# Expert rows gathered by token number: one layer of a hybrid attention, RG-LRU and MoE encoder

## The reference, cut to what matters

```python
g_sel = argmax(x @ w_router_group + b_router_group)            # 1 of 4 groups
e_logits = (x @ w_router_expert + b_router_expert)[group g_sel]  # 4 experts in it
top_vals, top_idx = top_k(e_logits, 2)
p_exp = softmax(top_vals) * p_group                            # gates of the two experts
for e in range(16):
    g, u = split(x @ w_gate_up[e])                             # 1024 -> 2 * 256
    y = y + gate[:, e] * ((silu(g) * u) @ w_down[e])           # 256 -> 1024
tokens = layer_norm(ALPHA * tokens + y)
```

## Time and profile before

| | |
|---|---|
| time, median of 3 runs | 1664.73 us (1663.65 to 1673.5) |
| the profiled execution's own time | 1661.35 us |
| its span in the trace | 1659.5 us |
| TensorE matrix products busy | 1496.0 us, 90% of the span |
| VectorE, ScalarE, POOL busy | 876.7, 531.9, 434.4 us |
| mean granted clock of TensorE | 0.956 of full speed |
| moved by DMA | 204.08 MB, mean 123 GB/s |

### The profile page before, as it was taken

How to read it: one execution, slowest core, us unless ns; L and a number is a source line. 1 busy time by engine, 2 the same in 40 slices (tenths; PEclk the granted TensorE clock), 3 DMA queues, 4 the chain that set the end, 5 groups by cost and what they waited for, 6 DMA issues and landing times.

```text
span 1659.5 us, 24972 instructions
## 1 busy us (share of the span) xinstructions
PE 1496.0 (90%) x10014; PEld 1344.0 (81%) x10014; DVE 876.7 (53%) x1648; ACT 531.9 (32%) x960; POOL 434.4 (26%) x465
## 2 busy tenths in 40 slices
PE   5989999999999899899999998999994299999990
PEld 5976679899999567789899897999994288888880
DVE  4025827999996577431546465443265034434445
ACT  4224542211111565520465655011011022222225
POOL 0744534813233000013334343231100302111110
PEclk7999999999999899999999999999998599999995
DMA  5111010232232830853111111244015768888946
GB/s 190 37 30 29 26 45 16 66 114 82 81 105 72 247 87 25 314 178 91 35 46 42 45 36 47 88 170 150 30 77 200 277 209 228 247 249 277 265 120 247
DMA packets 138089, 204.08 MB, mean 123 GB/s; under 512 B 14676, under 2 KB 89396, under 8 KB 137984
## 3 DMA queue, kind: packets, MB, share of 16 engines
q1 hardware_dynamic: 131808, 180.53, 33.6%
q0 software_dynamic: 6176, 22.10, 5.6%
HBM read 143.99 MB, written 58.61 MB: 122 GB/s over the span
## 4 chain that ended last, share of the span: by engine, by line
PE 76%; DMA 10%; DVE 5%; POOL 4%; issue 2%; ACT 2%; SPq 1%; POOLq 0%; DVEq 0%; ACTq 0%
PE psum L544 18%; PE psum L546 17%; PE psum L545 17%; DMA w_gate_up<-in_w_gate_up 5%; PE psum L1326 5%; PE psum L1140 3%; DMA x_and_experts_by_token<-expert_out,row_token 2%; PE psum L1130 2%; PE psum L1009 2%; PE psum L1162 2%; PE psum L1111 2%; POOL x_by_expert L935 1%; PE psum L1278 1%; PE psum L1318 1%; POOL roped L899 1%
## 5 line engine op out<-in xcount | busy, mean ns | idle before, releaser
L544 PE MATMUL psum<-x_hi,ring_hi 128*128 128x384 f32 x768 | 259.0, 337 | 0.5 <-ACT v L1518 0.5
L546 PE MATMUL psum<-x_lo,ring_hi 128*128 128x384 f32 x768 | 256.6, 334 | 0.0
L545 PE MATMUL psum<-x_hi,ring_lo 128*128 128x384 f32 x768 | 256.5, 334 | 0.0
L905 POOL CAST ring_hi<-ring_raw 128x512 fp32r<-128x512 f32 x88 | 67.1, 763 | 582.3 <-PE psum L546 415.8
L1326 PE MATMUL psum<-expert_rows_T,w_gate_up 128*128 128x192 f32 x1024 | 176.4, 333 | 13.2 <-DMA w_gate_up<-in_w_gate_up 11.8
L1326 PEld LDWEIGHTS psum<-expert_rows_T,w_gate_up 128*128 128x128 f32 x1024 | 171.9, 195 | 17.5 <-issue 8.4
L544 PE MATMUL psum<-w_hi,x_hi 128*128 128x256 f32 x576 | 174.0, 302 | 6.5 <-DVE channel_vectors L1781 3.7
L545 PE MATMUL psum<-w_hi,x_lo 128*128 128x256 f32 x576 | 165.3, 287 | 0.0
L546 PE MATMUL psum<-w_lo,x_hi 128*128 128x256 f32 x576 | 165.1, 287 | 0.0
L544 PEld LDWEIGHTS psum<-x_hi,ring_hi 128*128 128x128 f32 x768 | 144.2, 188 | 1.7 <-ACT v L1518 0.7
L545 PEld LDWEIGHTS psum<-x_hi,ring_lo 128*128 128x128 f32 x768 | 144.2, 188 | 1.1
(11 more groups left out here) (335 smaller groups left out, 3039.3 us busy)
## 6 DMA issues: line engine op xcount, KB each, us to landing
w_gate_up<-in_w_gate_up SPq DMA_DIRECT2D x16, 2048.0 KB, 14.1
ring_raw<-in_w_in SPq DMA_DIRECT2D x64, 256.0 KB, 3.4
w_down<-in_w_down SPq DMA_DIRECT2D x16, 1024.0 KB, 7.5
expert_rows<-x_by_expert SPq DMA_DIRECT2D x16, 774.0 KB, 5.5
x_by_expert<-zeros SPq DMA_DIRECT2D x7, 1536.0 KB, 16.2
gate_sigmoid<-sigmoid_out SPq DMA_DIRECT2D x15, 576.0 KB, 3.2
w_raw<-in_w_in SPq DMA_DIRECT2D x16, 512.0 KB, 4.4
k_cache<-in_cache_k SPq DMA_DIRECT2D x8, 1024.0 KB, 6.0
```

The costliest lines, as they stand in the source:

```text
L544: nc.tensor.matmul(out, ah, bh, start=first, stop=False)
L545: nc.tensor.matmul(out, al, bh, start=False, stop=False)
L546: return nc.tensor.matmul(out, ah, bl, start=False, stop=last)
L905: link(g.tensor_copy(RHI[:, p_ % 2, :, :], RRAW[:, p_ % 2, :, :]))
```

## The change

- x1 is stored a second time, by token, into a DRAM table X1D, whose row 0 is zero (token numbers begin with 1); the table of sums gets 96 more spare rows. The row buffer XS, its zero fills, the scatter and the eight extra columns are gone.
- `route` gives each (token, choice) its position within its expert (POSF). `mark_slots` compares it with 0 to 191 (AT_SLOT, six instructions of 128 x 576). TensorE multiplies AT_SLOT with the 0/1 rows times token number: 36 products of 128x96 weights and 16 columns (`row_table`), then once more with the gates. The result is the token number and the gate of every slot of all 16 experts (GIDX, ROWT, ROWG).
- The running count over tiles is one scan in place of nine steps; the gates come after the token table.
- POOL gathers the rows of expert e + 2 from X1D with two indirect DMAs, ahead of the adds of expert e. SP loads weights only. `row_columns` is gone from VectorE's loop, which is written out; the wait on landed adds moves to `expert_out`, two experts later.

The diff, cut to its core (the old lines of `route`, tables and the branch for overflow are left out):

```diff
-    XS = nc.dram_tensor("x1_by_expert", (E * TOK, DP), f32, kind="Internal").ap()
-    XS_1 = XS[0:E * MS, :].rearrange("(e h p) d -> e p h d", e=E, h=2)
...
-    YSUM = nc.dram_tensor("x1_and_experts_by_token", (1 + TOK + MR, D), f32, kind="Internal").ap()
-    FILLS = [YSUM[1 + TOK:, :].rearrange("p (a b) -> p a b", b=256)]
...
-    FILLS += [flat[:, n * i // 8:n * (i + 1) // 8, :] for i in range(8)]
+    X1D = nc.dram_tensor("x1_by_token", (1 + TOK, D), f32, kind="Internal").ap()
+    YSUM = nc.dram_tensor("x1_and_experts_by_token", (1 + TOK + 2 * MR, D), f32, kind="Internal").ap()
+    FILLS = [YSUM[1 + TOK:1 + TOK + MR, :].rearrange("p (a b) -> p a b", b=256)]
+    FILLS += [YSUM[1 + TOK + MR:, :].rearrange("p (a b) -> p a b", b=256)]
+    FILLS += [X1D[0:1, :].rearrange("p (a b) -> p a b", b=256)]
...
+        lg, le = LG[:, :, 0:4], LG[:, :, 4:20].rearrange("p t (q i) -> p t q i", q=4)
+        lm, tmp, hot = G16[:, 0, :, :], G16[:, 1, :, :], G16[:, 2:4, :, :]
+        def over_experts(x):
+            return x.unsqueeze(3).broadcast_to([128, 2, TT, E])
         first_max(lg, G1[:, 0, :], G4[:, 3, :, :], G1[:, 1, :], G4[:, 0, :, :], PRIO[:, 16:20], 4)
         v.tensor_tensor(G4[:, 1, :, :], lg, bc(G1[:, 0, :], 4), ALU.subtract).then_inc(s_route_steps, 1)
...
+        link(v.tensor_scalar(G4[:, 3, :, :], G4[:, 0, :, :], 1.0, BIG, ALU.subtract, ALU.mult))
+        link(v.tensor_tensor(lm.rearrange("p t (q i) -> p t q i", q=4), le,
+                             G4[:, 3, :, :].unsqueeze(3).broadcast_to([128, TT, 4, 4]), ALU.add))
+        first_max(lm, G1[:, 6, :], tmp, G1[:, 7, :], hot[:, 0, :, :], PRIO[:, 0:16], 16)
+        link(v.scalar_tensor_tensor(lm, hot[:, 0, :, :], -3.0 * BIG, lm, ALU.mult, ALU.add))
+        first_max(lm, G1[:, 8, :], tmp, G1[:, 7, :], hot[:, 1, :, :], PRIO[:, 0:16], 16)
+        link(v.tensor_tensor(PER_E[:, :, :].rearrange("p e t -> p t e"), hot[:, 0, :, :], hot[:, 1, :, :], ALU.add))
+        v.tensor_tensor_scan(UPTO[:, :, :].rearrange("p e t -> p (e t)"), SMASK, PER_E[:, :, :].rearrange("p e t -> p (e t)"),
+                             0.0, ALU.mult, ALU.add).then_inc(s_route_steps, 1)
+        v.tensor_tensor(G1[:, 4, :], G1[:, 8, :], G1[:, 6, :], ALU.subtract).then_inc(s_route_steps, 1)
+        v.tensor_tensor(HOT_TOKEN[:, :, :, :], hot, over_experts(TOKEN[:, :].unsqueeze(1).broadcast_to([128, 2, TT])), ALU.mult)
+        dve.wait_ge(s_route_products, 1)
+        pos = PS[:, 5, 0:E * TT].rearrange("p (e t) -> p t e", e=E).unsqueeze(1).broadcast_to([128, 2, TT, E])
+        link(v.tensor_tensor(G16[:, 0:2, :, :], hot, pos, ALU.mult))
+        link(v.tensor_reduce(POSF[:, :, :], G16[:, 0:2, :, :], AX.X, ALU.add))
+        mark_slots(v)
+        dve.wait_ge(s_route_products, 2)
+        tokens = PS[0:MR, 2:4, 0:E]
+        v.tensor_copy(GIDX[:, :, :], tokens).then_inc(s_rows_known, 1)
+        link(v.scalar_tensor_tensor(ROWU[:, :, :], tokens, 0.0, SPARE[:, :].unsqueeze(2).broadcast_to([MR, 2, E]),
+                                    ALU.is_equal, ALU.mult))
+        v.tensor_tensor(ROWT[:, :, :], ROWU[:, :, :], tokens, ALU.add).then_inc(s_rows_known, 1)
+        dve.wait_ge(s_route_exp, 1)
         link(v.tensor_reduce(G1[:, 2, :], G4[:, 2, :, :], AX.X, ALU.add))
         link(v.reciprocal(G1[:, 3, :], G1[:, 2, :]))
...
+        dve.wait_ge(s_route_exp, 2)
         link(v.tensor_scalar(G1[:, 9, :], G1[:, 5, :], 1.0, ALPHA, ALU.add, ALU.mult))
         link(v.reciprocal(G1[:, 9, :], G1[:, 9, :]))
...
+        link(v.tensor_tensor(GATES[:, 0, :], G1[:, 9, :], G1[:, 3, :], ALU.mult))
+        link(v.tensor_tensor(GATES[:, 1, :], GATES[:, 0, :], G1[:, 5, :], ALU.mult))
+        link(v.tensor_reduce(NMAXF[:, :], PS[:, 5, TT * E:TT * E + E], AX.X, ALU.max))
+        v.tensor_tensor(HOT_GATE[:, :, :, :], hot, over_experts(GATES[:, :, :]), ALU.mult).then_inc(s_at_slot, 1)
+        v.tensor_copy(NMAX[:, :], NMAXF[:, :]).then_inc(s_rows_known, 1)
+        dve.wait_ge(s_route_products, 3)
+        link(v.tensor_copy(ROWG[:, :, :], PS[0:MR, 6:8, 0:E]))
+    def mark_slots(v):
         for c in range(2):
...
+            for t in range(0, TT, 3):
+                v.tensor_tensor(AT_SLOT[:, c, t:t + 3, :], IOTA.unsqueeze(1).broadcast_to([128, 3, MS]),
+                                POSF[:, c, t:t + 3].unsqueeze(2).broadcast_to([128, 3, MS]), ALU.is_equal).then_inc(s_at_slot, 1)
...
                 sp.wait_ge(s_x1, t + 1)
+                sp.dma_start(X1D[1 + 128 * t:1 + 128 * t + 128, :], YACC[:, t, 0:D]).then_inc(s_x1_kept, 16)
                 sp.dma_start(YSUM[1 + 128 * t:1 + 128 * t + 128, :], YACC[:, t, 0:D]).then_inc(s_sums_begun, 16)
...
-            sp.wait_ge(s_scat, 16 * 2 * TT)
-            for e in range(2):
-                sp.dma_start(XG[:, e, :, :], XS_1[e]).then_inc(s_expert_rows_loaded[e], 16)
...
-                if not isinstance(e, int) or e + 3 < E:
-                    sp.wait_ge(s_expert_rows_turned, 4 * e + 8)
-                    sp.wait_ge(s_row_columns, 2 * e + 4)
-                    sp.dma_start(XG[:, 1 - par, :, :], of(XS_1, e + 3)).then_inc(s_expert_rows_loaded[1 - par], 16)
                 if not isinstance(e, int) or e + 2 < E:
                     sp.wait_ge(s_down_lo, e + 1)
                     sp.dma_start(WD[par][:, :, :], of(WD_D, e + 2)).then_inc(s_down_loaded[par], 16)
                     sp.wait_ge(s_gate_up_products, e + 1)
                     sp.dma_start(WG[par][:, :, :], of(WG_D, e + 2)).then_inc(s_gate_up_loaded[par], 16)
...
-            sp.wait_ge(s_expert_rows_turned, 4)
-            sp.wait_ge(s_row_columns, 2)
-            sp.dma_start(XG[:, 0, :, :], of(XS_1, 2)).then_inc(s_expert_rows_loaded[0], 16)
...
+            def gather_rows(e, par, column, done):
+                for h in range(2):
+                    g.indirect_dma_start(XG[:, par, h, :], None, X1D, bass.IndirectOffsetOnAxis(GIDX[:, h, column:column + 1], 0)
+                                         ).then_inc(done, 16)
+            def add_rows(par, h, column, done):
+                g.indirect_dma_start(YSUM, bass.IndirectOffsetOnAxis(ROWT[:, h, column:column + 1], 0), YE[:, par, h, :], None,
+                                     compute_op=ALU.add).then_inc(done, 16)
             pool.wait_ge(s_fill, 16 * len(FILLS))
-            for t in range(TT):
-                for c in range(2):
-                    g.indirect_dma_start(XS, bass.IndirectOffsetOnAxis(SLOT[:, c, t:t + 1], 0), YACC[:, t, :], None
-                                         ).then_inc(s_scat, 16)
-            def add_rows(par, h, done):
...
+            pool.wait_ge(s_x1_kept, 16 * TT)
+            pool.wait_ge(s_states_stored, 16 * 4)
+            pool.wait_ge(s_rows_known, 1)
+            for e in range(2):
+                gather_rows(e, e, e, s_expert_rows_loaded[e])
+            pool.wait_ge(s_rows_known, 2)
             pool.wait_ge(s_sums_begun, 16 * TT)
             for e in range(E):
+                if e + 2 < E:
+                    pool.wait_ge(s_expert_rows_turned, 4 * e + 4)
+                    gather_rows(e + 2, e % 2, e + 2, s_expert_rows_loaded[e % 2])
                 wait(pool, s_expert_out_kept[1 - e % 2], 32 * ((e + 1) // 2))
                 for h in range(2):
                     pool.wait_ge(s_expert_out, 4 * e + 2 * h + 2)
-                    add_rows(e % 2, h, s_expert_out_kept[e % 2])
+                    add_rows(e % 2, h, e, s_expert_out_kept[e % 2])
...
-            pe.wait_ge(s_route_steps, 3)
-            mm(PS[:, 5, 0:TT * E], BEFORE[:, :], G16[:, 5, :, :].rearrange("p t e -> p (t e)"), start=True, stop=False)
-            mm(PS[:, 5, 0:TT * E], ONES[:, :], G16[:, 6, :, :].rearrange("p t e -> p (t e)"), start=False, stop=True)
-            mm(PS[:, 5, TT * E:TT * E + E], ONES[:, :], G16[:, 7, 0, :], start=True, stop=True).then_inc(s_route_replies, 1)
+            pe.wait_ge(s_route_steps, 2)
+            mm(PS[:, 5, 0:TT * E], BEFORE[:, :], PER_E[:, :, :].rearrange("p e t -> p (e t)"), start=True, stop=False)
+            mm(PS[:, 5, 0:TT * E], ONES[:, :], UPTO[:, :, :].rearrange("p e t -> p (e t)"), start=False, stop=True)
+            mm(PS[:, 5, TT * E:TT * E + E], ONES[:, :], UPTO[:, :, TT - 1:TT].rearrange("p e t -> p (e t)"),
+               start=True, stop=True).then_inc(s_route_products, 1)
+            def row_table(values, bank, c0, marked):
+                for c in range(2):
+                    for t in range(TT):
+                        if t % 3 == 0 and marked is not None:
+                            pe.wait_ge(s_at_slot, marked + 3 * c + t // 3 + 1)
+                        for h in range(2):
+                            last = mm(PS[0:MR, bank + h, c0:c0 + E], AT_SLOT[:, c, t, MR * h:MR * h + MR], values[:, c, t, :],
+                                      start=(c, t) == (0, 0), stop=(c, t) == (1, TT - 1))
+                return last
+            row_table(HOT_TOKEN, 2, 0, 0).then_inc(s_route_products, 1)
+            pe.wait_ge(s_at_slot, 7)
```

(64 more changed lines are left out.)

194 lines of the change are left out of this document (75 added, 119 removed).

## The result

The changed kernel takes 1721.39 us (median of 4 runs, 1714.26 to 1724.57) where the kernel before takes 1664.45 (median of 4): a ratio of 1.033, 95% interval 1.031 to 1.035. It is slower, where 1623 was forecast. Its profiled execution took 1720.58, with a span of 1718.7 against 1659.5: 59.2 more.

A forecast was written before the change was run, and what follows sets the result against it. TensorE, busy 90% of the span, was taken as the bound, losing time before the first turn and to w_gate_up. 24.2 + 1.0 + 16.1 = 41.3 off 1661.35 gave 1620.1, forecast as 1623 from the median; range 1613 to 1642.

The forecast's parts named there:

- C: Expert loop: waits for w_gate_up go, gathers late by 0.1 us for 14 experts; 16.1 us gained, 17.5 at most.
- rival one: Expert loop: gathers share DMA with weight loads, land in 7.6 us, each late by 1.4; 1641.6 us; chance 0.20.
- rival three: Turns of 14 experts: POOL's gather much dearer than a plain load, landing above 9.5 us; at 3.8 late 1719; chance 0.04.
- T: Expert loop: the end of the second half of expert e, from which starts of gathers and needs are counted.
- POOL can't start sooner: Expert loop: the argument given for rival one, whose late gathers had a chance of 0.20.
- A: Path from logits to the first turn of expert rows: 24.2 us gained, bounds 5.6 and 28.1.
- B: Clock of the first half expert: 1.0 us gained, between 0 and 2.1.
- the path to the counts: Routing, in A: VectorE's shorter chain gives TensorE its counts at 1272.6, 4.3 us earlier than before.
- the six marks: Routing, in A: VectorE's marks of 576 elements take 0.76 us each, the first at 1276.0, the sixth at 1279.7.
- the gate table decides: Routing, in A: the gate table ends at 1292.1, later than the gather at 1290.5, and sets the first turn.
- the lower bound of the token table: Routing, in A: TensorE ends the table with the last mark, near 1280.5, where 1282.5 was taken.
- A loss is excluded: First half expert, in B: it can't get slower, since TensorE is at the low clock there already.

The follow-up runs named there:

- e2: Changed kernel, with SP loading an expert's w_down and w_gate_up only after that expert's gathered rows have landed; 1637.11 us.
- e6: Changed kernel, with VectorE's one instruction for the low part of w_down split into four; 1688.03 us.
- e1: Changed kernel, with POOL gathering the rows of expert e + 3 in place of e + 2, a beat earlier; 1634.02 us, 0.980 of the kernel before.
- e5: e1 plus ten idle matrix products of 512 columns keeping TensorE at work ahead of the tables; 1626.71 us, 0.977 of the kernel before.
- e3: Changed kernel, with each add moving 16 rows of 96, the other 80 left out of the sums; 1718.78 us.

## Why the prediction was wrong

**C failed, in the landing of the gather.** Of the 100.5 us between the forecast (41.3 less) and the two profiles (59.2 more), C is 84.1. The step "A plain load takes 5.5, an add on POOL's own queue 6.5. I take 6.5" set a landing of 6.5; it is 9.2. The rows that I took it from were of transfers with little beside them, or with one weight load. Here `w_down` and `w_gate_up` of e + 2 go out within 1 us of the second half, which I named in rival one and priced at 7.6. e2 shows that these loads are the whole difference: 5.1 without them. The clock behind the waits, 1.9 a beat, stood in rival three only and at nothing in the forecast. The Trainium skill ("DMA: Bandwidth & Descriptors", Queues, rings and completion order) lets each DMA engine take turns between queues packet by packet; the trace agrees that the gather has to share (5.1 alone, 9.2 beside them), but it pays 4.1 us for it, where the half rate of rival one gave 2.1. The DMA queues' view says where the rest comes from: POOL's queue has 38.2% of the engines from 1461 to 1464 us and moves 0.35 MB, 51.6% from 1464 to 1467 and moves 0.42 MB, so 0.12 to 0.14 MB in a microsecond; with the loads held, in e2, it has 97.6% from 1461.9 to 1463 and moves 0.34 MB in these 1.1 us. Even alone it is slower than the 384 GB/s that rival one halved.

**C failed, too, in the start of the second half**, T - 1.1 from the scatters' distance of 1.27 us: it is T + 0.26, since VectorE's 2.29 us instruction stands across the first half (e6). The scatters that I took the 1.27 from ran with VectorE idle. The formula was right, two of its terms were not: with e2's terms, 0.27 + 5.08 - 5.3, it gives 0.05, and e2 has no wait there. And "POOL can't start sooner", in rival one, holds for the rows of e + 2 only: e1 asks for each expert's rows a beat sooner.

**Rival three came true, with the cause of rival one.** Its price, 3.8 us of lateness, and its time, 1719, are nearly what was measured (4.65 a wait on average; 1721.39); its extra 3.1 for the clock is 1.9. That its time is so near is luck in part: it has the loop lose 79.1, where 68.0 is measured, and what A, B and the end fall short of the forecast, 14.1 together, happens to make up for it. I gave it 0.04 because I saw no reason for a dear gather; by itself a gather is cheap (5.1), and it is dear beside the loads. (13 gathers are late and not 14: that of the third expert goes out with no add ahead of it.) The landing from which it decides was given as above 9.5 us with the second half at T - 1.1; at the measured start it is 8.1, and 9.2 is above that. A slack of zero (late by 0.1) on 14 repeated steps should have had more weight than 0.04 for the slow side: each microsecond of error was worth 14 us.

**A was mis-sized, by 9.6 of 24.2**, in the pair of weight load and product: 0.09 taken, 0.1625 measured, two tables of 72, 10.4 us. The eight pairs of the earlier trace rows ran at a granted clock of 1.00; the tables run at 1.2 GHz. The price that the Trainium skill ("TensorE: Matmul & The Clock Gate", LDWEIGHTS) gives, by an estimate from it 0.08 for 96 columns, agrees with the 0.09 of e5 at the high clock; at the low one the trace has 0.1625, twice that. Right were the path to the counts (6.56 us behind the logits, 6.5 forecast), the six marks (4.10, forecast 4.6), the gather ahead of the turn, and that the gate table decides.

(In the lower bound of the token table it should say that TensorE is never faster than the marks; its number stands.)

**B**: -0.5, outside 0 to 2.1; the clock is still down when the half expert begins (0.50 from 1307 to 1310 us). "A loss is excluded" was wrong, but where the same tables take 7.0 to 8.1 us from one profile to the next, one pair of profiles can't tell a B of this size.

**Right**: no wait for `w_gate_up`, the beat of 17.3 once the rows are there (e1), the fills, the stores and the tail's work costing nothing that TensorE's waits show. e1 gets the 32.6 us that A, B and C give with the rows in time (14.6 + 0.5, with its first half expert of 7.00, + 17.5) and keeps 30.4 of it, since the end takes 2.2 longer.

**Open**: the end behind the last add is 43.5 us here and 40.5 before. ScalarE waits 3.39 us for the second sums in place of the 1.50 before. With the same tail e5 takes 40.8 and e6 44.7, so the change need not be the reason. No run was made for it, nor for the moving start of the routing, nor for the lower clock of e3.

## What to carry to other kernels

A step with no slack that is repeated for each expert puts the whole loop at stake: work out what each microsecond of error costs before choosing between two rows, and read the price of a DMA from a row with the same loads beside it. When a load moves to another queue, list everything that goes out within its landing time, on all queues. Before paying for a faster transfer, issue it one beat earlier: that cost a few lines here and was worth 87 us (e1 against the changed kernel).
